# Forgetting gates computed in block 1, S5 outputs and transposes one chunk later, and the forget logits with activations stationary

## The reference

```python
u = rmsnorm(h, g_pre)
p = u @ w_in                        # 4096 x (12*1024 + 8)
(fq, fk, fv, fgate, f_logit, sq, sk, sv, sgate, su, ssm_gate, lx, lru_gate) = split(p)
log_f = log_sigmoid(f_logit + b_forget)      # 8 heads: the forgetting gates
# forgetting attention: scores + cumsum(log_f)[q] - cumsum(log_f)[k], causal softmax
# stick-breaking attention; S5 state space mixer with GELU and GLU; RG-LRU with conv4
# each of the four outputs times silu(its gate columns), concatenated
h + rmsnorm(mixed @ w_out, g_post)
```

## Time and profile before

| | |
|---|---|
| median of 3 runs | 1551.7 us (1551.67 to 1552.07) |
| the profiled execution, its own time | 1551.9 us |
| its span in the trace | 1550.0 us |
| PE busy | 1525.6 us, 98% of the span |
| DVE busy | 927.1 us, 60% |
| ACT busy | 858.8 us, 55% |
| mean granted TensorE clock | 0.997 |

### The profile page before, as it was taken

How to read it: one execution, slowest core, us unless ns; L and a number is a source line. 1 busy time by engine, 2 the same in 40 slices (tenths; PEclk the granted TensorE clock), 3 DMA queues, 4 the chain that set the end, 5 groups by cost and what they waited for, 6 DMA issues and landing times.

```text
span 1550.0 us, 22156 instructions
## 1 busy us (share of the span) xinstructions
PE 1525.6 (98%) x7090; PEld 1254.7 (81%) x7090; DVE 927.1 (60%) x1154; ACT 858.8 (55%) x1158; POOL 86.6 (6%) x130
## 2 busy tenths in 40 slices
PE   8999999999999999999999999999999999999996
PEld 7888887778877788888878888888888888888885
DVE  6544478899888895454554544455566444444445
ACT  6644476666776656566554445556666443444442
POOL 0000010111211110000000000000000000000000
PEclk9999999999999999999999999999999999999999
DMA  8466656665665665565655555555556866666675
GB/s 303 136 198 190 188 167 186 181 198 172 183 186 179 194 192 177 181 198 172 194 162 165 175 163 166 171 179 176 164 172 201 276 193 196 193 191 192 194 232 179
DMA packets 86104, 291.26 MB, mean 188 GB/s; under 512 B 9904, under 2 KB 13232, under 8 KB 86064
## 3 DMA queue, kind: packets, MB, share of 16 engines
q1 hardware_dynamic: 77328, 276.86, 59.3%
q10 hardware_dynamic: 8736, 13.89, 2.7%
HBM read 286.51 MB, written 4.19 MB: 188 GB/s over the span
## 4 chain that ended last, share of the span: by engine, by line
PE 90%; DVE 4%; issue 2%; ACT 2%; DMA 1%; SPq 0%; DVEq 0%; POOL 0%; ACTq 0%; POOLq 0%
PE main L261 28%; PE main L263 28%; PE main L262 27%; PE side L392 2%; DMA w_raw<-in_wall 1%; PE main L286 1%; DVE vals L1062 1%; PE side L354 1%; PE side L343 0%; DVE w_lo L843 0%; PE side L318 0%; ACT w_hi L519 0%; PE side L386 0%; PE side L409 0%; DVE vals L1068 0%
## 5 line engine op out<-in xcount | busy, mean ns | idle before, releaser
L843 DVE TENSOR_TENSOR w_lo<-w_raw,w_hi 128x1024 fp32r<-128x1024 f32 x512 | 634.6, 1243 | 581.6 <-ACT w_hi L519 580.9
L519 ACT ACTIVATE w_hi<-w_raw 128x1024 fp32r<-128x1024 f32 x512 | 540.5, 1058 | 604.9 <-PE main L263 586.1
L261 PE MATMUL main<-w_hi,acts 128*128 128x512 f32 x2032 | 803.3, 395 | 3.9 <-ACT cross L528 2.5
L263 PE MATMUL main<-w_hi,acts 128*128 128x512 f32 x2032 | 792.9, 390 | 0.0
L262 PE MATMUL main<-w_lo,acts 128*128 128x512 f32 x2032 | 791.9, 390 | 0.0
L261 PEld LDWEIGHTS main<-w_hi,acts 128*128 128x128 f32 x2032 | 382.2, 188 | 89.6 <-ACT cross L528 5.2
L263 PEld LDWEIGHTS main<-w_hi,acts 128*128 128x128 f32 x2032 | 381.9, 188 | 81.0
L262 PEld LDWEIGHTS main<-w_lo,acts 128*128 128x128 f32 x2032 | 382.4, 188 | 76.4
L1341 POOL TENSOR_TENSOR scr<-scr 128x256 f32<-128x256 f32 x32 | 31.3, 977 | 491.5 <-ACT scr L611 491.5
L1062 DVE TENSOR_TENSOR_SCAN vals<-small,vals 128x256 f32<-128x256 f32 x64 | 40.9, 680 | 0.0
L1364 POOL COPY scr<-br 128x256 f32 x16 | 12.3, 769 | 372.7 <-DVE head_sel L1169 309.9
(11 more groups left out here) (247 smaller groups left out, 744.8 us busy)
## 6 DMA issues: line engine op xcount, KB each, us to landing
w_raw<-in_wall SPq DMA_DIRECT2D x512, 512.0 KB, 3.6
br<-in_x SPq DMA_DIRECT2D x16, 256.0 KB, 7.9
scr<-in_wglu ACTq DMA_DIRECT2D x8, 512.0 KB, 3.5
out<-br SPq DMA_DIRECT2D x7, 512.0 KB, 2.7
br<-in_gpost ACTq DMA_DIRECT2D x8, 256.0 KB, 4.6
vals<-in_x ACTq DMA_DIRECT2D x8, 256.0 KB, 5.0
scr<-in_x ACTq DMA_DIRECT2D x8, 256.0 KB, 4.2
scr<-in_bt ACTq DMA_DIRECT2D x32, 32.0 KB, 2.6
```

The costliest lines, as they stand in the source:

```text
L261: pe.matmul(main[:, bank0 + a, :], u_h, wh, start=(k == 0), stop=False)
L263: mm = pe.matmul(main[:, bank0 + a, :], u_l, wh, start=False, stop=(k == NK - 1))
L519: act.activation(w_hi[:, c % RING, :], w_raw[:, c % RING, :], ACT.Copy).then_inc(hi_ready, 1)
L843: dve.tensor_tensor(w_lo[:, c % RING, :], w_raw[:, c % RING, :], w_hi[:, c % RING, :].bitcast(F32), ALU.subtract).then_inc(lo_ready, 1)
```

## The change

- The logits are computed with the activations stationary: for each half of the tokens and each of the 32 slices, one matmul of the high activations with 16 weight columns (8 high, 8 low parts) and one of the low activations with the 8 high columns, 128 matmuls in all (L321 and L323 of the changed kernel). The result comes in token rows, so the turning (L370) falls away.
- The whole rest of the chain (bias, `abs`, `exp`, `ln`, `logf`, running sums, bf16 parts) moves from the stretch after block 11 and block 16 into block 1, which each engine now has written out ahead of its loop over blocks 2 and 3. `dec_rows` gets a buffer of its own, `logf` and others another place.
- `C_AT` goes from 14 to 15: the S5 outputs and DVE's step behind them come one chunk later.
- In each gate block ACT does one SiLU of a single column at chunk 14, ahead of the two large ones after chunk 15.
- In blocks 20 to 23 the transposes and `copy_weights` come six chunks behind the scores, not five.

```diff
-        C_AT = CH - 2
+        C_AT = CH - 1
...
             pe.wait_ge(wf_lo, 1)
-            for k in range(NK):
-                mm = pe.matmul(side[:, 3, :], wf[:, 2 * k * FT:2 * k * FT + P], acts[:, k, :], start=(k == 0),
-                               stop=(k == NK - 1))
+            for a in range(TT):
+                at = a * 2 * FT
+                for k in range(NK):
+                    pe.matmul(side[:, 3, at:at + 2 * FT], acts[:, k, a * P:(a + 1) * P],
+                              wf[:, 2 * k * FT:2 * (k + 1) * FT], start=(k == 0), stop=False)
+                    mm = pe.matmul(side[:, 3, at:at + FT], acts[:, k, T + a * P:T + (a + 1) * P],
+                                   wf[:, 2 * k * FT:(2 * k + 1) * FT], start=False, stop=(k == NK - 1))
             mm.then_inc(fl_mm, 1)
...
             def src_block(i):
+                def forget_sums():
+
+                    pe.wait_ge(lf_ready, 3)
+                    pe.matmul(side[0:ROWS, 1, 0:P], logf[:, 0, :], upto[:, :], start=True, stop=True)
+                    pe.matmul(side[0:ROWS, 1, P:T], logf[:, 0, :], later[:, 0:P], start=True, stop=False)
+                    pe.matmul(side[0:ROWS, 1, P:T], logf[:, 1, :], upto[:, :], start=False,
+                              stop=True).then_inc(dec_mm, 1)
+
                 for c in range(CH):
                     if c == T_AT:
                         turn_rows(i - 1, i - 1)
+                    if c == 9 and isinstance(i, int):
+                        forget_sums()
                     chunk_in(i, c)
...
-            pe.wait_ge(side_free, FT + 1)
-            for a in range(TT):
-                mm = pe.matmul(side[:, 3, a * FT:(a + 1) * FT], fl_rows[0:2 * FT, a * P:(a + 1) * P], fl_sel,
-                               start=True, stop=True)
-            mm.then_inc(fl_mm, 1)
...
-                        if c == SB_AT[a] + 5:
+                        if c == SB_AT[a] + 6:
                             pe.wait_ge(at_exp, i * 2 + (2 * FT + a + 1))
                             transposes(h)
...
# ACT
+                    if c == 5 and isinstance(i, int):
+                        act.wait_ge(fl_dve, 3)
+                        act.activation(fl_e, fl_z, ACT.Abs).then_inc(fl_act, 1)
+                        act.wait_ge(fl_act, 2)
+                        act.activation(fl_e, fl_e, ACT.Exp, scale=-1.0).then_inc(fl_act, 1)
+                        act.wait_ge(fl_act, 3)
+                        act.activation(fl_e, fl_e, ACT.Ln, bias=1.0).then_inc(fl_act, 1)
+                    if c == 10 and isinstance(i, int):
+                        act.wait_ge(dec_mm, 1)
+                        act.activation(dec_rows, side[0:ROWS, 1, 0:T], ACT.Copy, scale=-1.0).then_inc(dec_neg, 1)
...
+                    if c == CH - 2:
+                        act.activation(small[:, 146:147], later[:, 0:1], ACT.Silu)
                     if c == CH - 1:
                         take_gate(i + B_G1)
...
# DVE
+                    if c == 4 and isinstance(i, int):
+                        forget_values()
+                    if c == 7 and isinstance(i, int):
+                        log_forgets()
+                    if c == 11 and isinstance(i, int):
+                        decay_rows()
```

More of the change, by code:

```diff
@@ L82, in hybrid_trunk @@
         head_sel = sb("head_sel", [P, 2], BF16)
+        dec_rows = sb("dec_rows", [96, T], BF16)[:, :]
         ident = sb("ident", [P, P])
@@ L419, in fox_block @@
                         turn_rows(i + (B_G1 - 1), i + (T_GATE - 1))
[L420 to L425, removed]
                     for a in range(2):
@@ L594, in _ @@
             act.wait_ge(fl_mm, 1)
-            act.activation(fl_cross[0:2 * FT, :], side[0:2 * FT, 3, T:2 * T], ACT.Copy).then_inc(fl_act, 1)
+            act.activation(fl_cross, side[:, 3, 0:2 * TT * FT].rearrange("p (a r n) -> p a r n", a=TT, r=2)[:, :, 1, :],
+                           ACT.Copy).then_inc(fl_act, 1)
             def load_inputs(f):
@@ L614, in _, with src_block @@
             load_inputs(0)
-            with act.Fori(1, B_QK - B_SRC) as i:
+            def src_block(i):
                 for c in range(CH):
@@ L620, in _ @@
                         take_turned(i - 1)
+                    if c == 5 and isinstance(i, int):
[8 more added lines that the diff above has]
+                        act.activation(dec_rows, side[0:ROWS, 1, 0:T], ACT.Copy, scale=-1.0).then_inc(dec_neg, 1)
                     if c == CH - 1:
                         take_rows(i, in_rows, ACT.Copy, rstd)
+            src_block(1)
+            with act.Fori(2, B_QK - B_SRC) as i:
+                src_block(i)
             turns(0, 0)
@@ L1012, in _ @@
             dve.wait_ge(fl_act, 1)
-            dve.tensor_tensor(fl_rows[0:2 * FT, :], side[0:2 * FT, 3, 0:T], fl_cross[0:2 * FT, :],
-                              ALU.add).then_inc(side_free, 1)
+            dve.tensor_tensor(fl_sum, side[:, 3, 0:2 * TT * FT].rearrange("p (a r n) -> p a r n", a=TT, r=2)[:, :, 0, :],
+                              fl_cross, ALU.add).then_inc(fl_dve, 1)
             def take_s5(f):
@@ L1025, in _, with forget_values, log_forgets, decay_rows @@
             take_s5(0)
-            with dve.Fori(1, B_QK - B_SRC) as i:
+            def forget_values():
+                dve.wait_ge(fl_dve, 1)
+                for a in range(TT):
+                    dve.scalar_tensor_tensor(fl_z[:, a, :], fl_sum[:, a, :], rstd[:, a:a + 1],
+                                             col("b_forget")[:, a * FT:(a + 1) * FT], ALU.mult,
+                                             ALU.add).then_inc(fl_dve, 1)
+                dve.memset(logf, 0.0).then_inc(fl_dve, 1)
+            def log_forgets():
+                dve.wait_ge(fl_act, 4)
+                dve.wait_ge(fl_dve, 4)
+                for n in range(3):
+                    dve.scalar_tensor_tensor(logf[:, :, 32 * n:32 * n + FT], fl_z, 0.0, fl_e, ALU.min,
+                                             ALU.subtract).then_inc(lf_ready, 1)
+            def decay_rows():
+                dve.wait_ge(dec_neg, 1)
+                dve.scalar_tensor_tensor(dec_r1, side[0:ROWS, 1, 0:T], -1.0, dec_rows, ALU.mult,
+                                         ALU.subtract).then_inc(dec_dve, 1)
+                dve.wait_ge(dec_dve, 1)
+                dve.tensor_scalar(dec_mid, dec_r1, 1.0, None, ALU.mult).then_inc(dec_dve, 1)
+                dve.wait_ge(dec_dve, 2)
+                dve.tensor_tensor(dec_r2, dec_r1, dec_mid, ALU.subtract).then_inc(dec_dve, 1)
+                dve.tensor_scalar(dec_rows[32:64, :], dec_mid[32:64, :], 1.0, None, ALU.mult).then_inc(dec_dve, 1)
+                dve.wait_ge(dec_dve, 3)
+                dve.tensor_scalar(dec_rows[64:96, :], dec_r2[64:96, :], 1.0, None, ALU.mult).then_inc(side_free, 1)
+            def src_block(i):
                 for c in range(CH):
                     low(i, c + LEAD)
+                    if c == 4 and isinstance(i, int):
[4 more added lines that the diff above has]
+                        decay_rows()
+            src_block(1)
+            with dve.Fori(2, B_QK - B_SRC) as i:
+                src_block(i)
             dve.wait_ge(t_free, FT // JB)
@@ L1085, in _ @@
             s5_block(B_V - B_QK - 1)
[L1088 to L1093, removed]
             dve.wait_ge(t_free, B_QK)
@@ L1137, in head_out @@
                 dve.tensor_scalar(br[:, FOX0 + h, :], side[:, 2, 0:T], 1.0, None, ALU.mult).then_inc(at_o, 1)
[L1141 to L1161, removed]
             def fox_block(i):
```

27 lines of the change are left out of this document (7 added, 20 removed).

## The result

The changed kernel takes 1558.3 us (median of 6 runs, 1557.92 to 1559.61) against 1551.7 us for the kernel before (6 runs, 1549.9 to 1552.19). The ratio is 1.0047, with its 95% interval 1.0034 to 1.006: slower by 5 to 9 us. The profiled execution also took 1558.3 us, with a span of 1556.5 us and a mean granted clock of 0.991.

A forecast was written before the change was run, and what follows sets the result against it. PE, busy 98% of the span, was taken as the bound, so only its work and waits count. Profiled 1551.9 us, less 11.5 of gains, plus 0.8 and 17.6 of costs, gave 1558.8, as median 1558.6; range 1546.5 to 1561.5.

The forecast's parts named there:

- The fall of the clock: Narrow logit passes, end of block 0: clock drops to 1.2 GHz 5 us in (3.7 to 7); forecast's chance 0.50.
- (c): S5 outputs one chunk later: a 1.2 us wait and 0.17 in six blocks go; gain 2.2 us, bounds 0 to 2.2.
- the logits: End of block 0: 128 narrow passes with slow matmuls behind take 25.0 us instead of 7.4, costing 17.6 us.
- (a): After block 11: the turning of the logits falls away, gain 0.7 us.
- (b): Block 16: running sums leave, 2.8 us with 2.0 of wait, and 1.7 us of slow clock behind; gain 4.5 us.
- (d): Gate blocks: table load one chunk earlier removes four PE waits of 2.5 us and their edges; gain 3.5 us (3.0 to 3.6).
- (e): Block 23: later transposes remove a 0.8 us wait, a 0.3 wait before the values replaces it; gain 0.6 us (0 to 1.0).
- sums in block 1: Running sums moved into block 1 cost PE 0.8 us there, with their inputs early and no wait.
- rival 1: End of block 0: clock stays up, narrow logits cost only 6.7 us more; 1547.7 us in all, chance 0.40.
- rival 3: Later S5 outputs make PE wait at the inputs of seven blocks, 0.5 us each, 3.5 in all; chance 0.06.
- Rival 4: Block 16: gains hidden by a new wait for `low`, delayed by DVE's long multiply; under 1 us, no chance given.
- Rival 2: Narrow logit passes far cheaper than a load, near 0.03 us each; 1537.6 us in all, chance 0.04.

The follow-up runs named there:

- experiment 8: The kernel before, with only the running sums of the log gates moved from chunk 1 to chunk 2 of block 16: 1548.0 us against 1551.2, ratio 0.998.
- experiment 5: Against wide, the S5 outputs put back from chunk 15 to chunk 14: 1543.6 us, ratio 0.9954 to the kernel before.
- experiment 6: Against wide, the one-column SiLU at chunk 14 of the gate blocks removed: 1546.1 us, ratio 0.997 to the kernel before.
- experiment 7: Against wide, transposes and copies of the stick-breaking heads put back to five chunks behind the scores: 1543.1 us, ratio 0.995 to the kernel before.
- wide: The changed kernel with the logits in their old form, 32 matmuls with 512 moving columns, all else as changed: 1542.1 us against 1550.1, ratio 0.9947.
- Experiment 9: Against wide, DVE's skip term at chunk 15 of each S5 block put ahead of that chunk's remainder step: 1541.7 us, ratio 0.9942 to the kernel before.

## Why the prediction was right, step by step

The forecast of 1558.6 us was 0.3 above the median measured, by the mechanism it named. That it came so near is luck in two ways. The fall of the clock, worth 10 us, was chosen at 0.50 against 0.40. And two terms were too large by 1.0 us each, one a gain and one a cost, (c) and the logits, so that they cancel. The ledger by steps, in us of PE's stream:

| step | predicted | measured | from |
|---|---|---|---|
| (a) turning | 0.7 | 0.7 | trace after |
| (b) sums and aftermath in block 16 | 4.5 | 4.5 | traces before and after; experiment 8: 3.9, with 0.7 left for the sums |
| (c) S5 outputs | 2.2 | 1.2 | trace after; experiment 5: 1.3 |
| (d) table load | 3.5 | 3.5 | trace before; experiment 6 |
| (e) transposes | 0.6 | 0.7 | trace after; experiment 7 |
| sums in block 1 | -0.8 | -0.7 | trace after |
| logits | -17.6 | -16.6 | 7.4 to 24.0 |
| sum | -6.9 | -6.7 | the spans, 1550.0 and 1556.5, give -6.5 |

What the column leaves out are delays of a few hundredths in the starts behind each place.

**The logits.** Three separate statements were made. A pass costs what its load costs: right, 0.11 at the upper level and 0.21 at the lower (0.22 expected from the earlier trace rows). The clock falls about 5 us into the stretch: 5.2 in the one profile. The slow block matmuls behind it cost 1.7: measured 1.7. The term came out 1.0 too large, mainly because 80 passes ran slowly and not 83, at 0.213 each and not 0.22. That the clock falls at all was a choice at nearly even odds and not a reading.

Two readings behind this were less firm than they look. The windows of the profile give a granted clock of 1.00 around, so the lower level there was inferred from the spacing alone. What speaks for it is that the same 30 bf16 matmuls take 1.84 us in the profile of wide, where the 3.39 of the earlier trace rows are nearly twice that. And the lower bound of the moment, 3.7 us, was misread. The window just ahead of the earlier trace rows has

```profile
798.00:799.00 1.00, 1.00 (x6) 0.82 (x5) 1.00 (x3) 0.43 (x1) 0.00 (x0) 0.76 0.00 0
```

so about half of that microsecond ran at each level, and the clock fell near 798.5, 3.4 us after the stream broke off.

Experiments 2 and 4 show why the fall was hard to foresee: with the same passes and 128 columns moving, or with the same columns in portions of 16 passes, the clock stays up, and the time is that of rival 1 (1547.7 worked out; 1548.2 and 1548.6 measured). In the profile of before no stretch of loads was long enough to show it.

A rule of the Trainium skill stood behind rival 1: "TensorE: Matmul & The Clock Gate", in its table on what matters for kernels, asks to keep TensorE busy continuously and to leave no long idle gaps. In the changed kernel PE had no idle time from 62 to 84 us and the granted clock was 0.50 from 70 on. So in this case the measurement decides against taking "busy" as enough: what the busy engine does counts too.

The same page, section LDWEIGHTS, lets a load take its columns divided by 1.2, in nanoseconds, which is 107 for 128 columns. The 0.11 of the upper level agrees. At the lower level the loads came 0.21 apart, which that formula doesn't tell.

**Step (c) is the one that was mis-sized.** The gain itself was right (1.2 for the wait, 0.12 to 0.17 in six blocks), and rival 3 named what could take it back. But the prediction gave DVE a slack of 1.0 us, worked out as if DVE had caught up before chunk 15, with only `high` and `low` of the last chunk between PE's last chunk and the skip term. That holds in block 5, where 1.1 us are left. In blocks 6 to 10 DVE does its four last chunk steps without a pause, and 0.35 us are left. In block 4 the skip term ends 3.6 us after PE begins chunk 15 (265.18 to 268.82), in block 5 1.8 us after (313.00 to 314.81); the 1.8 us between them are more than the slack, and PE waited 0.72. A part of this comes with the step itself. In the kernel before, PE's own wait of 1.2 us gave DVE time: its last scan of block 4 ended at 245.3 and PE began chunk 15 at 249.2, 3.9 us later. In the changed kernel these are 262.7 and 265.2, 2.5 us. The prediction worked the slack out from rows that had this wait in them. Experiment 9 confirms the place: with the skip term one step earlier the wait disappears.

**The other steps.** Step (e): the new wait worked out as 0.3 is seen as a delay of 0.2 at the values. Rival 4 had no effect: `low` at the end of block 16 makes nobody wait. Rival 2 is refuted by the spacing of the loads in every kernel with narrow passes.

Not settled: what decides the moment of the fall. It came 5.2 us into the stretch with 16 and 8 columns and 3.3 us with 64, in one profile each.

## What to carry to other kernels

Here a matmul with a stationary operand of 128 columns of its own cost its weight load, 0.11 us, with 8, 16 or 128 columns moving. So cutting the moving columns that far saved nothing: count the loads before swapping operands. A long run of such passes can also bring the clock down though the engine is never idle: put them in portions between wide matmuls, or keep the wide form. When a step is moved to the last chunk, take its slack from the block in which the engine behind it is furthest behind, and ask whether a wait that the change removes was what gave that engine its time.

## What the runs showed of the hardware

- Of four kernels with 128 back-to-back passes or portions of them, the granted clock was 1.00 throughout with 128 columns moving and with portions of 16 narrow passes, and 0.50 for most of the stretch with 64 columns and with 16 and 8. The mean clocks of all their executions agree: 0.997 or 0.998 in 20, 0.989 to 0.991 in ten.
- Doing more work made the kernel faster: 128 columns in place of 16 and 8 took 1548.2 instead of 1558.3 us, since they are hidden behind the loads and the clock stays up.
- The start spacing of weight loads of 128 columns goes with the clock: 0.11 us at 1.00, 0.21 at 0.50.
- A wait of 2.0 us on PE in block 16 cost 3.9 us in the profiled execution (experiment 8).
- Going back and forth between the stream and 16 narrow passes costs nothing beyond the passes: 1.8 us for 16 times 0.11.
